# A steps with the scores first and the output projection's wait for y's low part moved to its second pass, in a hybrid attention layer on one core

## The chip, the cores and the metric

The kernel runs on one core of a Trainium2 chip. Times are microseconds (us) on the device, from the first to the last instruction of a launch with what lies around them. The profile is one execution; the median is that of three others.

## The reference

One layer with a sequence of 1024 tokens and a model width of 1024, all in float32. Cut to what is computed:

```
h  = rmsnorm(x, pre_g)
aq, ak, av, ag, bq, bk, bv, bg = split(h @ w_in)
# A: 8 heads of 64, keys shared by 4 heads, chunks of 64 tokens, each sees itself and the one before
s  = aq . ak * scale - slope * |i - j|        # masked before the start
ya = (softmax of [s, sink] without the sink's column) @ av * silu(ag)
# B: 4 heads with two softmax maps each, blocks of 128 queries, all keys up to their chunk
p  = softmax(bq . bk * scale - slope * |i - j|)
yb = rmsnorm((p[0] - lam * p[1]) @ bv, subln_g) * (1 - lambda_init) * silu(bg)
y  = concat(ya, yb) @ w_out
return x + rmsnorm(y, post_g)
```

## The kernel before

**Three passes.** Every projection in full precision is made of three products: high times high, low times high, high times low, where `x_hi` is x rounded to the TensorE's fp32r and `x_lo` the rest. ScalarE (ACT) makes the high parts by a copy, VectorE (DVE) or GpSimd (POOL) the low ones by a subtraction.

**Stages.** First x is normed, transposed and split into `hT_hi`, `hT_lo`, and the values of both groups are projected. Then comes the long middle: the 21 other column groups of `w_in` (the units: queries and keys of B, `qB` and `kB`, of A, `qA` and `kA`, and gates `gB`, `gA`) are projected in *pieces* of 4 matmuls of 512 columns, 6 pieces to a half unit of 512 tokens, and the attention is interleaved with these pieces. Last comes the output projection, tile by tile of 128 tokens, into 4 banks of PSUM, with norm, residual and store.

**One list orders all engines.** `make_schedule` writes one list of steps, `SCHEDULE`; each engine walks through that same list and issues its own instructions of each step, in that order, with waits on semaphores. So whatever step stands earlier in the list stands earlier in every engine's queue. The main loop goes over slots: 24 units of B, then the 8 units of A (slots 24 to 31), then the last 8 of B. In slot n stand the scores of unit n and the transposes and values of unit n - 1, "the pair one back". `take(k)` puts the next k pieces of projection into the list; `PIECES_BESIDE` says how many belong to a slot. When a piece ends a half unit, `store` is put there (ACT copies or activates the PSUM result), and the DVE's share (`store_low` for `qB` and `kB`, `gate` for the gates) waits in `later` until the next `vector_parts()`.

**A unit of A** is a pair of chunks, 2p and 2p + 1, called even and odd here:
- `a_scores`: PE makes 16 small matmuls (L1253); DVE adds the bias and takes the minimum, 8 operations (L1066) and one small one per chunk (L1073).
- `a_exp`: ACT, 4 exponentials of a chunk (L839) and one of the sink (L842).
- `a_weights`: DVE adds and inverts the sums (L1079, L1082), POOL multiplies the weights (L695).
- `a_transpose`: PE transposes a chunk's weights (L1261) into the half bank `turned`; ACT copies them out (L850). PE may only write the odd chunk's when ACT has copied the even one's (`turned_read`): there is one `turned`.
- `a_values`: PE (L1273), then DVE moves the result to `qT_A` (L1087).

**In a store** a half of `kB` costs ACT 4 copies (L781) and DVE 4 subtractions (L980), one of `qB` 2 and 2 (L773, L975), one of a gate one tanh (L794) and two products (L992, L999). The DVE's share waits for all ACT copies of that half. `split` is ACT's high part of the next unit's weights (L730).

**The end.** `y_split` makes y's high part on ACT (L860) and its low part on DVE (L1095). `out_project` (L1290) runs hi x hi, lo x hi, hi x lo.

Of the kernel before, what the change touches and what calls it, by code (L numbers as in the profile page):

```python
# [42 lines left out]
TILES = SEQ // P  # L43
# [29 lines left out]
PIECES = 6  # L73
# [5 lines left out]
Y_PARTS = 3  # L79
# [6 lines left out]

PIECES_BESIDE = ([9, 4, 3, 4, 4, 5, 3, 7] + [5, 5, 2, 3, 6, 5, 2, 8] + [5, 5, 3, 4, 3, 5, 3, 6]
                 + [6, 6, 6, 6, 6, 5, 5, 5]
                 + [4, 7, 7, 6, 3, 6, 5, 5] + [6, 1, 5])

SCORES_FIRST = {1, 2, 3, 10, 11, 17, 18, 37}
PIECE_BETWEEN = {16, 36, 37}
# [11 lines left out]
def make_schedule():  # L104

    steps, later, held = [], [], []
    pieces = [(n, half, p) for n in range(NU) for half in range(2) for p in range(PIECES)]
    at = 0

    def take(count):  # L110
        nonlocal at
        for n, half, p in pieces[at:at + count]:
            if half == 0 and p == 0 and n + 2 < NU:
                steps.append(("split", n + 2))
            steps.append(("project", n, half, p))
            if half == 0 and p < LOWS and n + 2 < NU:
                steps.append(("low", n + 2, p))
            if p < PIECES - 1:
                continue
            kind, head = UNITS[n]  # L120
            if kind == "kB" and head and ("b_scores", head * TILES - 1) not in steps:
                held.append((n, half))
            else:
                store(n, half)
        at = min(at + count, len(pieces))

    def store(n, half):


        steps.append(("store", n, half))  # L130
        if n not in PLAIN:
            later.append(("gate" if n in GATES else "store_low", n, half))

    def vector_parts():
        steps.extend(later)
        later.clear()

    order = [("b", u) for u in range(3 * TILES)] + [("a", p) for p in range(STEPS_A)]  # L140
    order += [("b", u) for u in range(3 * TILES, B_UNITS)]
    place = {unit: n for n, unit in enumerate(order)}
    turns = {}
    for unit, n in place.items():
        turns.setdefault(n + 1, []).insert(0, unit)

    steps += [("split", 0), ("split", 1)]
    take(FIRST_PIECES)
    vector_parts()
    for slot in range(len(order) + 3):  # L150
        kind, now = order[slot] if slot < len(order) else (None, None)
        count = PIECES_BESIDE[slot]
        last = order[slot - 1] if 0 < slot <= len(order) else (None, None)
        if last[0] == "b":
            steps.append(("b_mix", last[1]))
        before = order[slot - 2] if 2 <= slot < len(order) + 2 else (None, 0)
        finishing = before[0] == "b" and before[1] % 4 == 3
        if finishing:
            steps.append(("b_finish", before[1] // 4))
        if last[0] == "a":  # L160
            steps.append(("a_weights", 2 * last[1] + 1))
        turning = sorted(turns.get(slot, []))
        first = [("b_transpose", unit, 0) if which == "b" else ("a_transpose", 2 * unit)
                 for which, unit in turning[:1]]
        if kind == "b":
            assert {("kB", now // TILES), ("qB", now // TILES)} <= set(UNITS[:at // (2 * PIECES)])
            first.append(("b_scores", now))
        elif kind == "a":
            first.append(("a_scores", now))
        if slot in SCORES_FIRST:  # L170
            first.reverse()
        steps += first[:1]
        if slot in PIECE_BETWEEN and len(first) == 2:
            take(1)
            count -= 1
        steps += first[1:]
        vector_parts()
        for n, (which, unit) in enumerate(turning):
            if n:
                steps.append(("b_transpose", unit, 0))  # L180
            if which == "b" and unit % TILES >= 4:
                if n or kind is None:
                    take(1)
                    count -= 1
                steps.append(("b_transpose", unit, 1))
            if kind == "b" and n == len(turning) - 1:
                if now % TILES == TILES - 1:
                    for later_n, half in held:
                        store(later_n, half)
                    held.clear()  # L190
                steps.append(("b_exp", now))
            if which == "a":
                take(1)
                count -= 1
                if kind == "a":
                    steps.append(("a_exp", 2 * now))
                steps.append(("a_transpose", 2 * unit + 1))
            now_taken = 2 if which == "a" else 1 + finishing
            take(now_taken)
            count -= now_taken  # L200
            if kind == "a":
                if which == "b":
                    steps.append(("a_exp", 2 * now))
                steps += [("a_exp", 2 * now + 1), ("a_weights", 2 * now)]
            steps.append((f"{which}_values", unit))
            if which == "b" and unit % 4 == 3:
                steps.append(("b_square", unit // 4))
        if kind == "b" and not turning:
            steps.append(("b_exp", now))
        take(1)  # L210
        count -= 1
        vector_parts()
        if finishing:
            steps.append(("b_finish_transpose", before[1] // 4))
        take(max(0, count))
    last = (NU - 1) * 2 * PIECES
    outs = list(range(KT))
    while at < len(pieces):
        take(1)
        vector_parts()  # L220
        if outs and at % OUT_EVERY == 0:
            steps.append(("split_out", outs.pop(0)))
        if at == last + PIECES + 1:
            steps += [("y_split", 0), ("y_split", 1)]
    steps += [("split_out", k) for k in outs]
    for t in range(TILES):
        if t + 2 < TILES:
            steps.append(("y_split", t + 2))
        steps += [("out_project", t, 0), ("out_project", t, 1), ("post", t)]
    return steps  # L230
# [5 lines left out]
def hybrid_layer(nc, x, w_in, w_out, pre_norm_g, post_norm_g, sinks, lambda_q1, lambda_k1,  # L236
# [27 lines left out]
    a_weights = [place("a_weights0", 148.25, [P, 2, A_PAIRS, P]), place("a_weights1", 144.25, [P, 2, A_PAIRS, P])]  # L264
# [286 lines left out]
    with nc.Block() as block:  # L551
# [571 lines left out]
        def _(pe):  # L1123
# [51 lines left out]
            for step, *i in SCHEDULE:  # L1175
# [56 lines left out]
                elif step == "b_finish_transpose":  # L1232
                    f = i[0]
# [30 lines left out]
                elif step == "a_values":  # L1264
                    p = i[0]
                    pe.wait_ge(turned_read, turned_count("a_transpose", 2 * p + 1))
                    pe.wait_ge(mixed_read, mixed_before((step, *i)))
                    for e in range(2):
                        v = v_sb[:, p, B_WIDTH:V_WIDTH] if e else v_shift[:, p, :]
                        to = mixed[:, 256 * e:256 * e + 256]  # L1270
                        for h in range(2):
                            part = slice(HEAD_DIM * h, HEAD_DIM * (h + 1))
                            last = nc.tensor.matmul(to[part, :], v[:, part], a_weightsT[:, e, 2 * h:2 * h + 2, :],  # L1273
                                                    start=True, stop=True)
                    last.then_inc(a_valued, 1)
                elif step == "out_project":
                    t, half = i
                    tokens, cols = slice(P * t, P * t + P), slice(HALF * half, HALF * half + HALF)
                    pe.wait_ge(y_lo_ready, Y_PARTS * (t + 1))
                    if t >= 2:  # L1280
                        pe.wait_ge(y_weighted, 2 * (t - 2) + half + 1)
                    at = 1024 * (t % 2) + HALF * half
                    for p, (y, w) in enumerate(((hT_hi, wo_hi), (hT_lo, wo_hi), (hT_hi, wo_lo))):
                        for k in range(KT):
                            if t == 0 and half == 0 and p != 1:
                                if p:
                                    pe.wait_ge(wo_lo_ready[k % 2], k // 2 + 1)
                                else:
                                    pe.wait_ge(wo_hi_ready, k + 1)
                            last = nc.tensor.matmul(scores[:, at:at + HALF], y[:, k, tokens], w[:, k, cols],  # L1290
                                                    start=(p == 0 and k == 0), stop=(p == PASSES - 1 and k == KT - 1))
                    last.then_inc(out_projected, 1)
# [19 lines left out]
```

## Time and profile before

| | |
|---|---|
| median of 3 runs | 533.04 us (530.73 to 533.13) |
| profiled execution, its own time | 530.51 us |
| its span | 528.7 us |
| PE busy | 507.7 us, 96% |
| DVE busy | 263.5 us, 50% |
| ACT busy | 250.8 us, 47% |
| POOL busy | 115.6 us, 22% |
| TensorE's granted clock, mean | 0.995 |
| HBM read, written | 27.40 MB, 4.19 MB |

PE's busy time is close to the span, so the table says that work on PE, or a wait of PE, is what a change has to touch. It does not say where PE waits, nor what would be late next: for that the rows below are read, which show when each engine did what in a step of A and at the start of the output projection.

### The profile page before, as it was taken

To read this page: it belongs to the slowest core of one execution; us is meant where nothing else is said; L and a number is where in the kernel's file an instruction comes from. 1 tells how busy PE (TensorE), PEld (TensorE's weight loads), DVE (VectorE), ACT (ScalarE), POOL (GpSimd) and SP (SyncE) were. 2 spreads that over 40 slices of the span, in tenths; PEclk is the share of its full clock that TensorE was granted. 3 is DMA by queue.
4 is the path that set the end of the run, shared out by engine and by line. 5 is a ranking of instruction groups with operands and counts; after the bars stand their busy time and mean duration, and the time that the engine had idled before them with its cause. 6 is when DMAs were issued, how large, how long until landed. Compare 5 with 4: busy or idle time off the path is not lost.

```text
span 528.7 us, 7554 instructions
## 1 busy us (share of the span) xinstructions
PE 507.7 (96%) x2776; PEld 426.0 (81%) x2776; DVE 263.5 (50%) x642; ACT 250.8 (47%) x614; POOL 115.6 (22%) x154
## 2 busy tenths in 40 slices
PE   6999999999999999999999999989999999999995
PEld 5899997888878787888886767768788878888884
DVE  3656002465575556445547778445554475443332
ACT  5454213466476456556478666623645371221211
POOL 3410404040222120323043244222302260000000
PEclk9999999999999999999999999999999999999999
DMA  8730005120101110110101110111000653332222
GB/s 295 230 121 2 1 16 142 41 65 16 40 3 38 42 41 0 41 40 2 41 5 37 41 40 1 42 40 40 2 1 0 160 160 120 103 131 85 81 79 79
DMA packets 41300, 32.57 MB, mean 62 GB/s; under 512 B 18544, under 2 KB 35888, under 8 KB 41264
## 3 DMA queue, kind: packets, MB, share of 16 engines
q1 hardware_dynamic: 38960, 27.89, 18.9%
q10 hardware_dynamic: 2304, 4.20, 2.1%
q8 instruction: 22, 0.36, 0.3%
q14 instruction: 14, 0.11, 0.1%
HBM read 27.40 MB, written 4.19 MB: 60 GB/s over the span
## 4 chain that ended last, share of the span: by engine, by line
PE 80%; ACT 5%; DVE 4%; DMA 4%; issue 4%; POOL 2%; SPq 1%; DVEq 0%; POOLq 0%; ACTq 0%
PE proj L1188 35%; PE scores L1290 14%; PE proj L1158 10%; PE scores L1207 6%; PE banks L1228 5%; PE banks L1218 3%; DMA wo_early<-in_w_out 2%; PE banks L1273 2%; PE scores L1253 1%; PE banks L1261 1%; PE scores L1131 1%; DMA w_raw<-in_w_in 1%; DMA pre_g<-in_pre_norm_g 1%; ACT weights L801 1%; ACT k_stack L781 1%
## 5 line engine op out<-in xcount | busy, mean ns | idle before, releaser
L640 POOL TENSOR_TENSOR w_lo<-w_raw,w_hi 128x256 fp32r<-128x256 f32 x84 | 60.9, 754 | 184.8 <-ACT w_hi L730 184.8
L1188 PE MATMUL proj<-hT_hi,w_hi 128*128 128x512 f32 x336 | 89.9, 400 | 0.8 <-DVE k_stack L980 0.6
L1188 PE MATMUL proj<-hT_hi,w_lo 128*128 128x512 f32 x336 | 89.4, 400 | 0.0
L1188 PE MATMUL proj<-hT_lo,w_hi 128*128 128x512 f32 x336 | 88.5, 400 | 0.0
L1035 DVE CUSTOM_DVE_ANT_0 weights<-scores,dist_b 128x128 f32<-128x128 f32 (+7 forms) x64 | 45.9, 754 | 53.9 <-PE scores L1207 53.8
L1188 PEld LDWEIGHTS proj<-hT_hi,w_hi 128*128 128x128 f32 x336 | 60.5, 188 | 14.1 <-DVE k_stack L980 1.0
L1188 PEld LDWEIGHTS proj<-hT_hi,w_lo 128*128 128x128 f32 x336 | 60.6, 188 | 13.3 <-issue 1.9
L1188 PEld LDWEIGHTS proj<-hT_lo,w_hi 128*128 128x128 f32 x336 | 60.6, 188 | 11.8 <-issue 0.8
L801 ACT ACTIVATE weights<-weights,small 128x128 f32<-128x128 f32 (+7 forms) x64 | 49.0, 767 | 14.9 <-DVE small L1035 14.9
L811 ACT ACTIVATE weightsT<-banks 128x512 f32<-128x512 f32 (+3 forms) x48 | 23.6, 491 | 58.3 <-PE banks L1218 58.2
L1207 PE MATMUL scores<-k_stack,q_stack 128*128 128x512 f32 (+3 forms) x192 | 41.8, 353 | 0.0
L1228 PEld LDWEIGHTS banks<-v_sb,weightsT 128*128 128x128 f32 x288 | 36.2, 191 | 4.5 <-ACT weightsT L811 1.9
L1228 PE MATMUL banks<-v_sb,weightsT 128*128 128x128 f32 x288 | 37.8, 276 | 0.1
L644 POOL TENSOR_TENSOR small<-small 128x1 f32<-128x1 f32 (+1 forms) x24 | 17.2, 717 | 87.1 <-DVE small L1108 85.7
L1207 PEld LDWEIGHTS scores<-k_stack,q_stack 128*128 128x128 f32 x192 | 31.9, 189 | 4.8 <-DVE k_stack L980 0.4
L870 ACT ACTIVATE banks<-scores 128x512 f32<-128x512 f32 x16 | 9.3, 582 | 54.7 <-PE scores L1290 54.7
L1290 PE MATMUL scores<-wo_hi,hT_hi 128*128 128x512 f32 x128 | 31.7, 390 | 1.3 <-DVE hT_lo L1095 1.3
L1019 DVE SCALAR_TENSOR_TENSOR weights<-weights,small,weights 128x512 f32<-128x512 f32 (+3 forms) x48 | 31.1, 676 | 1.1
L1290 PE MATMUL scores<-wo_lo,hT_hi 128*128 128x512 f32 x128 | 31.6, 389 | 0.0
L1290 PE MATMUL scores<-wo_hi,hT_lo 128*128 128x512 f32 x128 | 31.6, 389 | 0.0
L1066 DVE CUSTOM_DVE_ANT_0 a_weights<-scores,dist_a,small 128x128 f32<-128x128 f32 x64 | 22.5, 406 | 17.9 <-PE scores L1253 17.9
L1290 PEld LDWEIGHTS scores<-wo_hi,hT_hi 128*128 128x128 f32 x128 | 23.9, 188 | 6.6 <-DVE hT_lo L1095 1.7
(106 smaller groups left out, 721.8 us busy)
## 6 DMA issues: line engine op xcount, KB each, us to landing
w_raw<-in_w_in SPq DMA_DIRECT2D x13, 512.0 KB, 3.9
x_in<-in_x SPq DMA_DIRECT2D x8, 512.0 KB, 5.9
w_raw<-in_w_in SPq DMA_DIRECT2D x16, 256.0 KB, 3.5
x_res<-in_x SPq DMA_DIRECT2D x8, 512.0 KB, 4.4
out<-y_out ACTq DMA_DIRECT2D x16, 256.0 KB, 2.3
wv_raw<-in_w_in SPq DMA_DIRECT2D x2, 640.0 KB, 7.4
wo_early<-in_w_out SPq DMA_DIRECT2D x4, 256.0 KB, 4.9
w_raw<-in_w_out SPq DMA_DIRECT2D x4, 256.0 KB, 6.2
```

Source lines behind the costliest of these rows:

```text
L640: nc.gpsimd.tensor_tensor(w_lo[:, n % SPLIT, k], w_raw[:, n % RAW, k], w_hi[:, n % SPLIT, k].bitcast(F32), ALU.subtract).then_inc(w_lo_rea ...
L644: nc.gpsimd.tensor_tensor(out_, in_, neg_half[:, 0:width], ALU.pow).then_inc(done, 1)
L801: nc.scalar.activation(w, w, ACT.Exp, scale=-1.0, bias=min_b[:, 2 * u + m:2 * u + m + 1], accum_out=sum_b[:, 2 * u + m:2 * u + m + 1]).the ...
L811: nc.scalar.activation(weightsT[:, 4 * r:4 * r + blocks, :], turned[:, 0:P * blocks].rearrange("p (b q) -> p b q", q=P), ACT.Copy).then_in ...
L1019: nc.vector.scalar_tensor_tensor(w0, w1, mix_b[:, u:u + 1], w0, ALU.mult, ALU.add).then_inc(b_mixed, 1)
L1035: nc.vector.tensor_tensor_reduce(out=weights_1[:, 0:keys] if m else weights_0[:, u % 2, 0:keys], in0=scores[:, 1024 * m:1024 * m + keys], ...
L1066: nc.vector.tensor_tensor_reduce(out=a_weights_of(c)[:, j, :], in0=scores[:, a_scores_at(c, j):a_scores_at(c, j) + P], in1=dist_a[:, min(c ...
L1158: last = nc.tensor.matmul(proj[:, n % 2, 0:VG], h[:, k, tokens], w[:, k, cols], start=(p == 0 and k == 0), stop=(p == PASSES - 1 and k == ...
L1188: last = nc.tensor.matmul(to, w[:, slot, k, :], h[:, k, HALF * half:HALF * half + HALF], start=(p == 0 and k == first), stop=(p == PIECES ...
L1207: last = nc.tensor.matmul(scores[:, 1024 * m + first:1024 * m + first + width], q_stack[head][m][:, P * block_:P * block_ + P], k[:, m, fi ...
L1228: last = nc.tensor.matmul(mixed[:, P * (u % 4):P * (u % 4) + P], weightsT[:, b, :], v_sb[:, b, P * head:P * head + P], start=(b == 0), sto ...
L1290: last = nc.tensor.matmul(scores[:, at:at + HALF], y[:, k, tokens], w[:, k, cols], start=(p == 0 and k == 0), stop=(p == PASSES - 1 and k ...
```

## The change

In slots whose transposes are those of an A unit (25 to 32), the list is written in another order. Before: transposes of the even chunk, scores of the new unit, the vector parts, a piece, exp of the new even chunk, transposes of the odd chunk, two pieces, exp of the new odd chunk, values, a piece, vector parts, other pieces. Now: scores, vector parts, two pieces, exp of the new even chunk, transposes of the even chunk, a piece, transposes of the odd chunk, exp of the new odd chunk, a piece, values, a piece, vector parts, other pieces. The count of pieces of a slot stays, but for one that moves from slot 33 to slot 32. In the output projection the wait for `y_lo_ready` stands at the second pass; the first waits for `y_hi_ready`.

```diff
-                 + [4, 7, 7, 6, 3, 6, 5, 5] + [6, 1, 5])
+                 + [5, 6, 7, 6, 3, 6, 5, 5] + [6, 1, 5])
...
+        if turning and turning[0][0] == "a":
+            done = turning[0][1]
+            steps.append((f"{kind}_scores", now))
+            vector_parts()
+            take(2)
+            steps += [("a_exp", 2 * now) if kind == "a" else ("b_exp", now), ("a_transpose", 2 * done)]
             take(1)
-            count -= 1
...
+            steps.append(("a_transpose", 2 * done + 1))
+            if kind == "a":
+                steps += [("a_exp", 2 * now + 1), ("a_weights", 2 * now)]
+            take(1)
+            steps.append(("a_values", done))
+            count -= 4
+        else:
...
-            if which == "a":
...
-                if kind == "a":
-                    steps.append(("a_exp", 2 * now))
-                steps.append(("a_transpose", 2 * unit + 1))
-            now_taken = 2 if which == "a" else 1 + finishing
...
                 elif step == "out_project":
...
-                    pe.wait_ge(y_lo_ready, Y_PARTS * (t + 1))
+                    pe.wait_ge(y_hi_ready, Y_PARTS * (t + 1))
...
                     for p, (y, w) in enumerate(((hT_hi, wo_hi), (hT_lo, wo_hi), (hT_hi, wo_lo))):
+                        if p == 1:
+                            pe.wait_ge(y_lo_ready, Y_PARTS * (t + 1))
```

The new code's line numbers are 4 higher on all engines in the middle stage (L980 is L984, L1066 is L1070), and 6 higher in the output projection.

The first place is the DVE's queue around the first half of unit 12, the keys of B's last head. Before, in slots 27 and 28 (from the end of the scores of unit 3 to the start of those of unit 4):

```order
L1073 TENSOR_TENSOR small<-small 128x4
L980 TENSOR_TENSOR k_stack<-proj,k_stack 64x512 x4
L1079 TENSOR_TENSOR small<-small 128x4
L1082 RECIPROCAL small<-small 128x4
L1087 TENSOR_SCALAR qT_A<-banks 128x2x256
L1079 TENSOR_TENSOR small<-small 128x4
L1082 RECIPROCAL small<-small 128x4
L1066 ISA a_weights_61,small<-scores,dist_a,small 128x128
```

The same operations of this half unit now, from the end of the scores of unit 2 to the start of those of unit 3:

```order
L1077 TENSOR_TENSOR small<-small 128x4
L1083 TENSOR_TENSOR small<-small 128x4
L1086 RECIPROCAL small<-small 128x4
L1091 TENSOR_SCALAR qT_A<-banks 128x2x256
L984 TENSOR_TENSOR k_stack<-proj,k_stack 64x512 x4
L1083 TENSOR_TENSOR small<-small 128x4
L1086 RECIPROCAL small<-small 128x4
L1070 ISA a_weights_62,small<-scores,dist_a,small 128x128
```

The four subtractions stood behind a slot's score operations (before) and stand now, a whole slot's score operations earlier, ahead of the odd chunk's inversion and of the scores of unit 3 (its weights lie in `a_weights_62`).

The second place is ACT's queue in the same slots, 27 and the start of 28. Before:

```order
L781 ACTIVATE k_stack<-proj 64x512 x4
L850 ACTIVATE a_weightsT<-banks 128x512
L839 ACTIVATE a_weights_62,small<-a_weights_62,small 128x128 x4
L842 ACTIVATE small<-small 128x4
L850 ACTIVATE a_weightsT<-banks 128x512
L839 ACTIVATE a_weights_62,small<-a_weights_62,small 128x128 x4
```

And now:

```order
L785 ACTIVATE k_stack<-proj 64x512 x4
L843 ACTIVATE a_weights_62,small<-a_weights_62,small 128x128 x4
L846 ACTIVATE small<-small 128x4
L854 ACTIVATE a_weightsT<-banks 128x512 x2
L843 ACTIVATE a_weights_62,small<-a_weights_62,small 128x128 x4
L846 ACTIVATE small<-small 128x4
```

Both copies of the transposed weights now stand behind the new unit's even exponentials; before, the even one stood ahead of them.

The third place is PE's queue in that slot, its projection pieces of 4 matmuls with it. Before:

```order
L1261 MATMUL banks<-ident,a_weights_61 128x128 x4
L1253 MATMUL scores<-kT_A,qT_A 128x128 x8
L1188 MATMUL proj<-hT_hi,w_hi 128x512 x4
L1261 MATMUL banks<-ident,a_weights_61 128x128 x4
L1188 MATMUL proj<-hT_lo,w_hi 128x512 x8
L1273 MATMUL banks<-a_weightsT,v_shift 64x256 x2
```

And now:

```order
L1257 MATMUL scores<-kT_A,qT_A 128x128 x8
L1192 MATMUL proj<-hT_hi,w_hi 128x512 x4
L1192 MATMUL proj<-hT_lo,w_hi 128x512 x4
L1265 MATMUL banks<-ident,a_weights_61 128x128 x4
L1192 MATMUL proj<-hT_lo,w_hi 128x512 x4
L1265 MATMUL banks<-ident,a_weights_61 128x128 x4
L1192 MATMUL proj<-hT_hi,w_lo 128x512 x4
L1277 MATMUL banks<-a_weightsT,v_shift 64x256 x2
```

The scores no longer stand between the two sets of transposes, and the distance from the odd chunk's transposes to the values is one piece instead of two.

## Rows read from the trace of the kernel before

**Rows 1.** The page's engine line of PE: busy us, share of the span, instructions.

```profile
PE 507.7 (96%) x2776; PEld 426.0 (81%) x2776; DVE 263.5 (50%) x642; ACT 250.8 (47%) x614; POOL 115.6 (22%) x154
```

**Rows 2.** Who PE waited for, 262 to 350 us: total, times, longest.

```profile
PE banks L1218 <- DVE weights L1019: 2.1, 1, 2.1
PE banks L1261 <- POOL a_weights L695: 1.9, 3, 1.2
PE banks L1273 <- ACT a_weightsT L850: 0.5, 1, 0.5
```

**Rows 3.** Timeline of PE, slots 27 and 32: start, us, what.

```profile
293.03 1.08 PE L1188 MATMUL proj<-hT_hi,w_hi 128*128 128x512 f32 x4
293.95 0.60 PE L1261 MATMUL banks<-ident,a_weights 128*128 128x128 f32 x4
294.48 1.26 PE L1253 MATMUL scores<-kT_A,qT_A 64*128 64x128 f32 x16
...
296.70 0.60 PE L1261 MATMUL banks<-ident,a_weights 128*128 128x128 f32 x4
297.05 2.09 PE L1188 MATMUL proj<-hT_lo,w_hi 128*128 128x512 f32 x8
299.07 0.65 PE L1273 MATMUL banks<-a_weightsT,v_shift 128*64 128x256 f32 x4
...
338.88 0.60 PE L1261 MATMUL banks<-ident,a_weights 128*128 128x128 f32 x4
339.24 0.64 PE L1207 MATMUL scores<-k_stack,q_stack 128*128 128x128 f32 x4
```

**Rows 4.** Timeline of DVE, slot 27, and the gate in slot 29.

```profile
295.89 0.41 DVE L1066 CUSTOM_DVE_ANT_0 a_weights<-scores,dist_a,small 128x128 f32<-128x128 f32 x1 [2.91 <-PE scores L1253]
...
298.95 2.84 DVE L980 TENSOR_TENSOR k_stack<-proj,k_stack 64x512 fp32r<-64x512 f32 x4
301.82 0.16 DVE L1079 TENSOR_TENSOR small<-small 128x4 f32<-128x4 f32 x1
...
302.23 0.69 DVE L1087 TENSOR_SCALAR qT_A<-banks 128x512 f32<-128x512 f32 x1
...
319.09 0.68 DVE L992 SCALAR_TENSOR_TENSOR gate<-gate,proj 128x512 f32<-128x512 f32 x1
...
320.42 0.15 DVE L1079 TENSOR_TENSOR small<-small 128x4 f32<-128x4 f32 x1
```

**Rows 5.** Timeline of ACT, slots 27, 29 and 32.

```profile
293.23 2.44 ACT L781 ACTIVATE k_stack<-proj 64x512 fp32r<-64x512 f32 x4 [2.61 <-PE proj L1188]
...
296.34 0.40 ACT L839 ACTIVATE a_weights<-a_weights,small 128x128 f32<-128x128 f32 x1
...
298.00 0.57 ACT L850 ACTIVATE a_weightsT<-banks 128x512 f32<-128x512 f32 x1
...
313.13 0.60 ACT L794 ACTIVATE gate<-proj 128x512 f32<-128x512 f32 x1 [2.63 <-PE proj L1188]
...
339.58 0.60 ACT L850 ACTIVATE a_weightsT<-banks 128x512 f32<-128x512 f32 x1 [2.09 <-PE banks L1261]
...
342.76 1.05 ACT L730 ACTIVATE w_hi<-w_raw 128x1024 fp32r<-128x1024 f32 x1
```

**Rows 6.** Timeline of POOL, slot 27.

```profile
302.27 1.04 POOL L695 TENSOR_TENSOR a_weights<-a_weights,small 128x512 f32<-128x512 f32 x1 [8.18 <-DVE small L1082]
```

**Rows 7.** Timeline of all engines where the output projection starts.

```profile
432.51 1.98 PE L1188 MATMUL proj<-hT_hi,w_lo 128*128 128x512 f32 x8
...
434.59 1.04 ACT L763 ACTIVATE wo_hi<-w_raw 128x1024 fp32r<-128x1024 f32 x1
435.02 0.68 DVE L1095 TENSOR_TENSOR hT_lo<-out_B,hT_hi 128x512 fp32r<-128x512 f32 x1
...
435.76 2.11 PE L1290 MATMUL scores<-wo_hi,hT_hi 128*128 128x512 f32 x8 [1.27 <-DVE hT_lo L1095]
...
436.90 1.21 DVE L1003 TENSOR_TENSOR wo_lo<-w_raw,wo_hi 128x1024 fp32r<-128x1024 f32 x1
```

More of the change, by code:

```diff
@@ L162, in make_schedule @@
         turning = sorted(turns.get(slot, []))
[L163 to L172, printed above, removed]
@@ L173, in make_schedule @@
-        if slot in PIECE_BETWEEN and len(first) == 2:
-            take(1)
-            count -= 1
[L176 to L191, printed above, removed]
-            if which == "a":
+        if turning and turning[0][0] == "a":
[4 more added lines that the diff above has]
+            steps += [("a_exp", 2 * now) if kind == "a" else ("b_exp", now), ("a_transpose", 2 * done)]
+            take(1)
+            steps.append(("a_transpose", 2 * done + 1))
[5 more added lines that the diff above has]
+        else:
+            first = [("b_transpose", unit, 0) for which, unit in turning[:1]]
+            if kind == "b":
+                assert {("kB", now // TILES), ("qB", now // TILES)} <= set(UNITS[:at // (2 * PIECES)])
+                first.append(("b_scores", now))
+            elif kind == "a":
+                first.append(("a_scores", now))
+            if slot in SCORES_FIRST:
+                first.reverse()
+            steps += first[:1]
+            if slot in PIECE_BETWEEN and len(first) == 2:
@@ L193, in make_schedule @@
                 take(1)
                 count -= 1
-                if kind == "a":
-                    steps.append(("a_exp", 2 * now))
-                steps.append(("a_transpose", 2 * unit + 1))
-            now_taken = 2 if which == "a" else 1 + finishing
-            take(now_taken)
-            count -= now_taken
-            if kind == "a":
-                if which == "b":
-                    steps.append(("a_exp", 2 * now))
-                steps += [("a_exp", 2 * now + 1), ("a_weights", 2 * now)]
@@ L205, in make_schedule @@
-            steps.append((f"{which}_values", unit))
-            if which == "b" and unit % 4 == 3:
-                steps.append(("b_square", unit // 4))
+            steps += first[1:]
+            vector_parts()
+            for n, (which, unit) in enumerate(turning):
+                if n:
+                    steps.append(("b_transpose", unit, 0))
+                if which == "b" and unit % TILES >= 4:
+                    if n or kind is None:
+                        take(1)
+                        count -= 1
+                    steps.append(("b_transpose", unit, 1))
+                if kind == "b" and n == len(turning) - 1:
+                    if now % TILES == TILES - 1:
+                        for later_n, half in held:
+                            store(later_n, half)
+                        held.clear()
+                    steps.append(("b_exp", now))
+                take(1 + finishing)
+                count -= 1 + finishing
+                if kind == "a":
+                    steps += [("a_exp", 2 * now), ("a_exp", 2 * now + 1), ("a_weights", 2 * now)]
+                steps.append((f"{which}_values", unit))
+                if which == "b" and unit % 4 == 3:
+                    steps.append(("b_square", unit // 4))
```

## The prediction

> **What bounds the kernel now.** I read the page first: PE is busy for 507.7 of 528.7 us [rows 1], so only a change of PE's work or of its waits moves the end. The other engines matter as what PE waits for. Then I asked the view of waits who PE waits for in the stretch of the A steps, 262 to 350 us [rows 2]: three waits for POOL's multiplied weights (1.9 us), one for ACT's copy of the transposed weights (0.5), one for the DVE's mixed weights of unit 24 (2.1). At the start of the output projection PE sits idle for 1.27 us until `hT_lo` is there [rows 7]. So 1.9 + 0.5 + 1.3 = 3.7 us is the most that the change can take away, unless it shortens PE's work, which it does not: the matmuls are the same. The 2.1 us before the transposes of unit 24 stay, because between the values of unit 7 and those transposes the list has one piece before and after, and the DVE's queue there is the same.
>
> **PE's clock through one new A slot.** I lay out a slot with 0 at the start of its scores, from the timelines. Before, scores and the piece behind them took 296.70 - 294.48 = 2.22 us, a plain piece 293.95 - 293.03 = 0.92, transposes 297.05 - 296.70 = 0.35, and a piece between two switches (299.07 - 297.05) / 2 = 1.01 [rows 3]. In the new order the even chunk's transposes start at 2.22 + 0.92 = 3.14, the odd chunk's at 3.14 + 0.35 + 1.01 = 4.50, the values at 4.50 + 0.35 + 1.01 = 5.86. Before, the odd chunk's transposes came at 2.22 and the values at 4.59.
>
> **The chain that must keep up.** The DVE starts the bias operations 295.89 - 294.48 = 1.41 after the scores start, if it is free [rows 3, 4]. ACT's first exponential starts 0.45 behind (296.34), and the chunk's five take 298.00 - 296.34 = 1.66 [rows 4, 5]. In the new list ACT has both copies of the transposed weights behind those exponentials; a copy takes 0.57 to 0.60, and starts 339.58 - 338.88 = 0.70 after its transposes [rows 3, 5]. PE may start the odd transposes only when the even copy is done. With a free DVE: exponentials done at 1.41 + 0.45 + 1.66 = 3.52, copy 3.84 to 4.44, odd transposes on time at 4.50. So the order just closes. Its slack is small: the odd transposes are late once the bias starts later than 4.50 - 0.05 (semaphore, chosen) - 0.57 - 1.66 - 0.45 = 1.77, or once anything else holds ACT past 3.9. From there every us of lateness is a us of PE idle, since nothing can pass in PE's queue.
>
> **What is late: the halves of kB.** Call E the issue of the group behind the last piece of a half unit. ACT begins the store at E + 0.20 (293.03, 293.23) and takes 2.44 for `kB` [rows 3, 5], so to E + 2.64. The DVE's four subtractions take 301.82 - 298.95 = 2.87 and the inversion 302.23 - 301.82 = 0.41 [rows 4]. In the new queue both stand ahead of the next scores: bias at E + 2.67 + 2.87 + 0.41 = E + 5.95. The next scores start one piece behind E, about E + 0.95, so the bias starts at 5.00 instead of 1.41, the exponentials end at 7.11, the copy at 7.68, and the odd transposes start at 7.73 instead of 4.50: **3.2 us** of idle PE. POOL's multiplication of the odd chunk (1.04 us, [rows 6]) ends about 6.1, inside that. Unit 12 is `kB`, with two halves stored in this stretch, in slots 26 and 27: 6.4 us in slots 27 and 28. Before, these subtractions stood behind the bias operations, where they delayed only the inversion of chunks that PE wanted later; what that cost is in [rows 2].
>
> **The other slots.** A gate's half takes ACT 0.60 and the DVE 320.42 - 319.09 = 1.33 [rows 4, 5]. With a piece between store and scores (slot 29) the bias starts at E + 0.83 + 1.33 + 0.41 = E + 2.57, or 1.62: inside the slack. In slot 30 no piece lies between, so the bias is at 2.57; ACT's exponentials start at 3.02 (the tanh, 0.60, and `w_hi`, 1.05, [rows 5], are over by 1.9), end at 4.68, and the odd transposes start at 5.30: 0.8 lost. In slot 31 a store lies between scores and exponentials; the tanh starts at 2.2 + 0.2 and pushes the exponentials' end to about 4.6 and the odd transposes to 5.2: 0.7. In slot 32 the same happens with scores of B, which are shorter (339.24, 0.64 of matmul time, [rows 3]), and `split` 17 stands between the two copies: 0.9. The `qB` half before slot 26 has half the operations of a `kB` half: bias near 1.9, 0.1 lost. Slots 24 and 25: nothing. Sum of new waits in A: 6.4 + 0.8 + 0.7 + 0.9 + 0.1 = 8.9.
>
> **What it removes.** The waits of [rows 2] for POOL and ACT, 2.4: multiplication and copy have a longer lead now.
>
> **Switching costs on PE.** Transposes directly before scores took 294.48 - 293.95 = 0.53, before a piece 0.35 [rows 3]: a switch from 128-row to 64-row operands costs about 0.18. The new order has that switch too, from a piece to the scores, and one more neighbourhood of a piece and transposes (1.01 against 0.92, 0.09). A piece ahead of scores does not occur in this trace. From below it costs no more than today's switch, 0; from above I take the 0.35 that the transposes themselves last, once per slot. I choose 0.5 us for the eight slots in all; ends 0 and 2.8. The Trainium skill, page "TensorEngine Tiling (Array Packing)", section "Key Properties", says that changing the tiling mode drains the TensorE. It gives no figure; the trace agrees that such a switch costs something (those 0.18 us), and behind the longer matmuls of a piece a drain would cost more than behind transposes, which is the upper end.
>
> **The output projection.** PE's last group before it starts at 432.51, and its eight matmuls issue in two plain pieces of 0.92, so PE is free at 432.51 + 1.84 = 434.35 [rows 3, 7]. The first pass needs y's high part, which must be over when its low part is being made, and `wo_hi`'s eight chunks; the last is ready at 434.59 + 1.04 = 435.63, and PE gets to it at 434.35 + 7 x 0.23 = 435.96. The second pass starts at 434.35 + 1.84 = 436.19; y's low part is ready at 435.02 + 0.68 = 435.70. `wo_lo`'s last chunk, 436.90 + 1.21 = 438.1, is wanted at 434.35 + 2 x 1.84 + 1.61 = 439.6 [rows 7]. All three covers hold, the first by 0.3 us only. Gain: 435.76 - 434.35 = **1.4**; ends 0.9 (chunk 7 late) and 1.4. Behind this PE runs to the end without a wait, so the gain stays.
>
> **Sum.** 8.9 + 0.5 - 2.4 - 1.4 = +5.6 us. Against the profiled execution's own 530.5 that is 536.1; the median of the runs shown is 2.5 higher, at 533.04, so I forecast 538.6 for the median. The stage behind A moves as a whole: its loads and stores wait on PE's own progress.
>
> **The rivals.**
> - *Faster.* The transposes' lead over their scores grows by a third, all waits of A go, and nothing takes their place: +0.5 - 2.4 - 1.4 = -3.3, 529.7. For it: the plain chain closes at 4.44 against 4.50. Against it: it needs the bias to start by 1.77 in every slot, and the DVE's queue puts the `kB` subtractions ahead. It would decide if those were done by E + 2.3, where even ACT's copies end at E + 2.64. Chance 0.09.
> - *Within 0.5%.* 0.5% is about what a measurement of this kernel can tell from no change, 2.7 us. The two `kB` waits come out at half and the small ones not at all: 3.2 + 0.5 - 2.4 - 1.4 = 0, 533; up to +2.6. For it: the small terms rest on a few tenths each. Against it: the `kB` chain is made of durations that hardly vary in the trace. Chance 0.13.
> - *The drain.* As forecast, but each scores block behind a piece costs the upper end: +2.3 more, 540.9. Chance 0.10.
> - *The output projection gains nothing*, because y's high part or chunk 7 comes as late as the low part did: +1.4, 540.0. The rows speak against it; chance 0.06.
> - The forecast, +3 to +7.5: chance 0.62.
>
> **How the numbers follow.** Faster 0.09, within 0.5% 0.13, slower 0.78 (0.62 + 0.10 + 0.06). The range: from a case with `kB` waits at half and one or two small ones (533.5, which takes in half of the middle case) to the forecast with the switching end (542). Left out: the faster case, the lower part of the middle one, and a little above.
>
> **What would show it.** In the new profile: the DVE's L984 x4 ahead of L1070 in slots 27 and 28 and its scores operations some 5 us behind PE's scores; PE idle about 3 us before L1265 twice, released by ACT's copy L854; under 1 us before L1265 three times; no wait for POOL; the stretch from the first A scores to the transposes of unit 24 longer by about 7 us; L1296 with no idle before it, and 1.4 us less between the last projection and the end. Wrong would be: no idle at L1265 (then the DVE's order does not reach PE), or idle before the scores L1257 themselves.

## The result and the profile after

| | before | changed |
|---|---|---|
| median of 6 runs each, same chip | 533.09 us | 539.84 us |
| lowest to highest | 530.73 to 533.23 | 537.86 to 540.85 |
| profiled execution, own time | 530.51 us | 537.86 us |
| its span | 528.7 us | 536.1 us |

The ratio is 1.0134, with a 95% interval of 1.0106 to 1.0162. It compares the means of the runs, which lie 7.1 us apart; the medians lie 6.75 apart and the two profiled executions 7.4. The forecast was 5.6 slower, a median of 538.6, with a range of 533.5 to 542.0.

The page's engine line of the changed kernel, beside [rows 1]:

```profile
PE 510.8 (95%) x2776; PEld 427.1 (80%) x2776; DVE 260.2 (49%) x642; ACT 250.5 (47%) x614; POOL 115.1 (21%) x154
```

The number of instructions is the same, but PE's busy time grew by 3.1 us. So not all of the loss is waiting; some matmuls took longer. Who PE waited for, in the whole run (total, times, longest), beside [rows 2], which cover the A stretch alone; of the second line here only the longest wait, 1.7, lies in that stretch:

```profile
PE banks L1265 <- ACT a_weightsT L854: 8.3, 5, 3.2
PE banks L1222 <- DVE weights L1023: 3.0, 4, 1.7
```

The row of POOL's multiplied weights is gone, and in its place stands ACT's copy of the transposed weights, five times. The timeline of PE in slots 26 and 27, beside [rows 3]:

```profile
289.04 0.63 PE L1265 MATMUL banks<-ident,a_weights 128*128 128x128 f32 x4
289.43 1.17 PE L1192 MATMUL proj<-hT_hi,w_lo 128*128 128x512 f32 x4
290.53 0.65 PE L1277 MATMUL banks<-a_weightsT,v_shift 128*64 128x256 f32 x4
...
292.58 1.07 PE L1192 MATMUL proj<-hT_hi,w_hi 128*128 128x512 f32 x4
293.58 1.26 PE L1257 MATMUL scores<-kT_A,qT_A 64*128 64x128 f32 x16
...
297.08 1.18 PE L1192 MATMUL proj<-hT_lo,w_hi 128*128 128x512 f32 x4
301.50 1.09 PE L1265 MATMUL banks<-ident,a_weights 128*128 128x128 f32 x4 [3.24 <-ACT a_weightsT L854]
302.24 2.06 PE L1192 MATMUL proj<-hT_hi,w_lo 128*128 128x512 f32 x4
304.22 0.93 PE L1277 MATMUL banks<-a_weightsT,v_shift 128*64 128x256 f32 x4
...
307.55 1.26 PE L1257 MATMUL scores<-kT_A,qT_A 64*128 64x128 f32 x16
```

Two things are to be seen. The odd transposes wait 3.24 us, released by ACT's copy. And behind the wait the same four matmuls take 2.06 us instead of 1.17: from the odd transposes to the next scores it is 307.55 - 301.50 = 6.05 us in slot 27 and 293.58 - 289.04 = 4.54 in slot 26, 1.51 more. The stretches' view says why; its columns are PE's busy time with its matmuls, then the weight loads, DVE, ACT, POOL, then the granted clock:

```profile
293.58:307.55 13.97, 10.73 (x57) 7.61 (x56) 7.11 (x27) 6.93 (x25) 2.08 (x2) 0.88 0.01 2
307.55:321.39 13.84, 10.61 (x57) 7.55 (x56) 7.47 (x28) 7.69 (x25) 4.87 (x6) 0.88 0.18 38
...
301.50:304.50 3.00, 3.00 (x10) 2.16 (x12) 0.41 (x3) 1.82 (x8) 1.04 (x1) 0.50 0.02 5
```

In slots 27 and 28 the granted clock is 0.88 on average, and 0.50, that is 1.2 GHz, right behind the wait. PE had been idle since 298.3; the clock was still 1.00 from 300 to 301, 0.91 from 301.0 to 301.5, and back at 1.00 from 305.0. The DVE and ACT in slot 27, beside [rows 4, 5], show where the wait comes from:

```profile
295.25 2.85 DVE L984 TENSOR_TENSOR k_stack<-proj,k_stack 64x512 fp32r<-64x512 f32 x4 [2.90 <-ACT k_stack L785]
298.13 0.16 DVE L1083 TENSOR_TENSOR small<-small 128x4 f32<-128x4 f32 x1
...
298.53 0.41 DVE L1070 CUSTOM_DVE_ANT_0 a_weights<-scores,dist_a,small 128x128 f32<-128x128 f32 x1
```

```profile
292.77 2.44 ACT L785 ACTIVATE k_stack<-proj 64x512 fp32r<-64x512 f32 x4 [0.78 <-PE proj L1192]
298.99 0.40 ACT L843 ACTIVATE a_weights<-a_weights,small 128x128 f32<-128x128 f32 x1 [3.77 <-DVE small L1070]
...
300.76 0.60 ACT L854 ACTIVATE a_weightsT<-banks 128x512 f32<-128x512 f32 x1
302.68 0.60 ACT L854 ACTIVATE a_weightsT<-banks 128x512 f32<-128x512 f32 x1 [1.33 <-PE banks L1265]
```

The scores start at 293.58 and their bias at 298.53, 4.95 later (forecast 5.00). ACT sits idle for 3.77 us in front of exponentials that stand ahead of a copy whose transposes have long been done. Where the output projection starts, beside [rows 7]:

```profile
440.41 0.69 DVE L1003 TENSOR_TENSOR out_B<-gate,out_B 128x512 f32<-128x512 f32 x1
440.51 2.85 POOL L683 TENSOR_TENSOR wo_lo<-w_raw,wo_hi 128x1024 fp32r<-128x1024 f32 x1 [1.82 <-ACT wo_hi L767]
...
441.40 1.98 PE L1192 MATMUL proj<-hT_hi,w_lo 128*128 128x512 f32 x8
441.64 2.33 DVE L1099 TENSOR_TENSOR hT_lo<-qT_A,hT_hi 128x256 fp32r<-128x256 f32 x2 [0.55 <-ACT hT_hi L864]
...
443.21 1.98 PE L1296 MATMUL scores<-wo_hi,hT_hi 128*128 128x512 f32 x8
```

Its first matmul follows 1.81 behind the start of the last group, against 435.76 - 432.51 = 3.25 before: 1.44 gained.

### The profile page after: what moved, and what is told of

It reads as the page before. It is cut to its first block, busy times and chain, and to the rows that moved or that the text cites. A ratio compares the mean times of both kernels' runs of the same rounds, so it can differ in the third digit from the quotient of the medians.

```text
span 536.1 us, 7554 instructions
## 1 busy us (share of the span) xinstructions
PE 510.8 (95%) x2776; PEld 427.1 (80%) x2776; DVE 260.2 (49%) x642; ACT 250.5 (47%) x614; POOL 115.1 (21%) x154
## 4 chain that ended last, share of the span: by engine, by line
PE 82%; ACT 6%; DVE 5%; issue 4%; DMA 2%; POOL 1%; SPq 0%; DVEq 0%; POOLq 0%; ACTq 0%
PE proj L1192 37%; PE scores L1296 14%; PE proj L1162 10%; PE scores L1211 6%; PE banks L1232 5%; PE banks L1222 3%; PE banks L1277 2%; DVE k_stack L984 2%; PE banks L1265 1%; ACT k_stack L785 1%; PE scores L1135 1%; PE scores L1257 1%; ACT a_weights L843 1%; DMA pre_g<-in_pre_norm_g 1%; DMA w_raw<-in_w_in 1%
## 5 line engine op out<-in xcount | busy, mean ns | idle before, releaser
L1192 PE MATMUL proj<-hT_hi,w_lo 128*128 128x512 f32 x336 | 92.1, 407 | 0.0
L1192 PE MATMUL proj<-hT_lo,w_hi 128*128 128x512 f32 x336 | 89.7, 400 | 0.0
L984 DVE TENSOR_TENSOR k_stack<-proj,k_stack 64x512 fp32r<-64x512 f32 x32 | 22.0, 688 | 18.2 <-ACT k_stack L785 17.5
L843 ACT ACTIVATE a_weights<-a_weights,small 128x128 f32<-128x128 f32 x64 | 24.8, 390 | 12.1 <-DVE small L1070 12.1
```

What stands on the lines that cost most here:

```text
L843: nc.scalar.activation(w, w, ACT.Exp, scale=-1.0, bias=min_a[:, s + j:s + j + 1], accum_out=sum_a[:, s + j:s + j + 1]).then_inc(a_exped, 1)
L984: nc.vector.tensor_tensor(k_lo[part, m, tokens], source[own, :], k_hi[own, m, tokens].bitcast(F32), ALU.subtract).then_inc(stack_lo, 1)
L1192: last = nc.tensor.matmul(to, w[:, slot, k, :], h[:, k, HALF * half:HALF * half + HALF], start=(p == 0 and k == first), stop=(p == PIECES ...
```

## The experiments

The ratios compare means with runs of the kernel before that were made beside the experiment's: 23 for experiments 1 to 4 (median 532.31 us), 17 for experiments 5 to 7 (532.32). The numbers of this section are the order in which the experiments are told.

**1. The DVE's share of a store behind the next scores again.**

```diff
         take(1)
         count -= 1
-        vector_parts()
+        if not (turning and turning[0][0] == "a"):
+            vector_parts()
```

> The changed kernel, but in slots that turn an A unit the DVE's share of a store is held back until behind the next scores, as it stood before the change. My theory (the DVE's queue order makes the two long waits, and the clock falls behind them): the two 3.2 us waits before the odd transposes go, and with them the stretches at a lower granted clock that follow them, about 1.5 us each; slot 30's 0.5 us goes too, slots 31 and 32 keep 0.6 each because there the store stands between scores and exponentials. Some 0.5 us may come in slot 28, where ACT has four k_stack copies and w_hi ahead of the exponentials. Together 9.4 to 9.9 us less than the changed kernel, so 530.0 to 530.5, ratio to before 0.994 to 0.996. Rival (scores first is itself dear, by the switch from a piece to 64-row scores and the short way from odd transposes to values): the waits shrink by less than half, ratio above 1.003.

Measured: 528.74 us (median of 6, 526.66 to 529.0), ratio to before 0.9925 (0.9901 to 0.9949). The profile's span is 524.9 us, 11.2 below the changed kernel. Its granted clock is 1.00 through the A stretch. Who PE waited for:

```profile
PE banks L1223 <- DVE weights L1024: 1.6, 4, 0.7
PE banks L1266 <- ACT a_weightsT L855: 1.6, 3, 0.7
```

One move of the DVE's instructions turns the change from slower than before to faster. Both long waits are gone; 0.30, 0.60 and 0.65 us are left before the odd transposes of slots 28, 31 and 32, as the theory had it. In the profiles it gained 11.2 us, where 9.4 to 9.9 were expected. Some 1.3 us of that were not in the theory: the wait before the transposes of unit 24 fell from 1.74 us to 0.42, because a gate's two products, 0.68 and 0.69 us on the DVE, no longer stand ahead of that unit's mix. The rival, scores first as such, is out.

**2. Both copies of the transposed weights ahead of the even exponentials.** The DVE's order stays as in the change.

```diff
-            steps += [("a_exp", 2 * now) if kind == "a" else ("b_exp", now), ("a_transpose", 2 * done)]
+            steps.append(("a_transpose", 2 * done))
             take(1)
             steps.append(("a_transpose", 2 * done + 1))
+            steps.append(("a_exp", 2 * now) if kind == "a" else ("b_exp", now))
```

> The changed kernel, but the even exponentials of the new unit stand behind both transposes of the old one in the list, so ACT copies the transposed weights first. The DVE's order stays as changed. My theory: the lateness reaches PE through two links, ACT's exponentials ahead of the copy (odd transposes possible at 7.7 us into the slot) and POOL's multiplication of the odd chunk (ends about 6.1 us into the slot). With the first link cut the second is left: 1.2 us of idle before the odd transposes in slots 27 and 28 each, released by POOL and not by ACT, and the small waits of slots 30 to 32 gone. If a wait of 1.2 us leaves the granted clock alone, 4.1 + 1.8 + 2.9 = 8.8 us less than the changed kernel: 531.0, ratio to before 0.996; if the clock still falls, 533.9, ratio 1.001. Rival (the DVE's lateness reaches PE by POOL alone, ACT's order does not matter): same as the changed kernel, ratio 1.013.

Measured: 533.13 us (median of 10), ratio 1.0025 (1.0009 to 1.0042), 5.8 us below the changed kernel's 1.0134. PE's waits in the two slots, from its timeline:

```profile
300.16 0.66 PE L1266 MATMUL banks<-ident,a_weights 128*128 128x128 f32 x4 [2.16 <-POOL a_weights L700]
...
312.40 0.66 PE L1266 MATMUL banks<-ident,a_weights 128*128 128x128 f32 x4 [1.41 <-POOL a_weights L700]
```

The theory's sign and place hold: ACT's link is cut, POOL's is left, and the small waits of slots 30 to 32 are gone. The rival that POOL alone carries the lateness is out. The size was missed: 2.16 and 1.41 us instead of 1.2 twice. Part of it is that ACT now does the exponentials later, which pushed the `kB` copies to 293.27, and the DVE's subtractions with them to 295.73, 2.41 us after the scores' start (1.67 in the changed kernel). The granted clock was 0.59 behind the longer wait and 1.00 behind the shorter one:

```profile
300.00:304.00 4.00, 3.84 (x16) 2.21 (x16) 2.43 (x16) 2.80 (x13) 0.20 (x2) 0.59 0.03 6
312.00:316.00 4.00, 3.60 (x21) 2.45 (x22) 3.07 (x19) 2.84 (x14) 2.55 (x5) 1.00 0.05 11
```

**3. The output projection's wait alone**, on the kernel before: only the last hunk of the change.

```diff
-                    pe.wait_ge(y_lo_ready, Y_PARTS * (t + 1))
+                    pe.wait_ge(y_hi_ready, Y_PARTS * (t + 1))
...
+                        if p == 1:
+                            pe.wait_ge(y_lo_ready, Y_PARTS * (t + 1))
```

> The kernel before with only the output projection's wait moved to its second pass. My theory: PE has no idle before the first matmul of the output projection, and 1.4 us less: 531.7, ratio 0.9973 (0.9968 to 0.998). Rival (something behind it gives it back, the y_weighted wait or the last norm): ratio 1.000.

Measured: 531.12 us (median of 12), ratio 0.9977 (0.9961 to 0.9993). A gain, but the profiled execution does not show it: its span is 528.8 us against 528.7 of the kernel before. It has waits that the theory did not have:

```profile
430.90 2.42 POOL L679 TENSOR_TENSOR wo_lo<-w_raw,wo_hi 128x1024 fp32r<-128x1024 f32 x1 [0.92 <-ACT wo_hi L763]
430.99 0.67 DVE L992 SCALAR_TENSOR_TENSOR gate<-gate,proj 128x512 f32<-128x512 f32 x1
431.70 2.18 DVE L999 TENSOR_TENSOR out_B<-gate,out_B 128x512 f32<-128x512 f32 x1
433.97 0.73 ACT L860 ACTIVATE hT_hi<-qT_A 128x256 fp32r<-128x256 f32 x2 [3.14 <-DVE out_B L999]
...
435.27 1.89 PE L1292 MATMUL scores<-wo_hi,hT_hi 128*128 128x512 f32 x7 [0.59 <-ACT hT_hi L860]
437.35 0.50 PE L1292 MATMUL scores<-wo_hi,hT_hi 128*128 128x512 f32 x1 [0.20 <-ACT wo_hi L763]
```

The DVE's product `out_B<-gate,out_B` takes 0.69 us in the changed kernel's profile and 2.18 here, where POOL's subtraction had begun 0.8 us ahead of it; it ends 0.56 us after POOL's does. In the changed kernel it began 0.10 us ahead of POOL's, and it was the DVE's next operations that took long (2.33 us for two, against 0.76 where POOL is quiet). So the high part of y comes early or late by which of the two engines is first. In the profiles of the kernel before, the changed kernel and experiment 1, the product began 0.06 to 0.14 us ahead of POOL; in those of experiments 2, 3, 4 and 5 POOL began 0.12 to 0.80 us ahead, and the product took 2.18 to 2.82 us. In experiment 3's profile the second pass starts 437.69 - 432.70 = 4.99 us behind the start of the last group, against 437.70 - 432.51 = 5.19 before, so only 0.2 us were gained there, and the first A scores had come 0.2 us later.

**4. The idle time filled**, to price the clock. The changed kernel computes what it did; 13 matmuls are added whose results nobody reads.

```diff
+                    if c in (5, 7):
+                        p = c // 2
+                        pe.wait_ge(a_biased, 2 * A_PAIRS * (p + 1))
+                        for f in range(FILL):          # FILL = 13
+                            nc.tensor.matmul(scores[:, 1024 * (p % 2):1024 * (p % 2) + HALF], hT_hi[:, f % KT, 0:P],
+                                             hT_hi[:, f % KT, 0:HALF], start=True, stop=True)
                     pe.wait_ge(a_weighted, c + 1)
```

> The changed kernel with 13 matmuls of 512 columns that nobody reads put on PE before the odd transposes in slots 27 and 28, where PE sits idle for 3.2 us; they write a bank of scores that is free then. The reads and waits of all else stay. My theory: the two waits cost more than their idle time, because the granted clock is lower behind them (0.88 over each slot); 13 matmuls take about 2.95 us and keep PE busy, so the granted clock stays at 1.00, the idle that is left is 0.3 us, and each slot is about 1.4 us shorter: 2.9 us less than the changed kernel, 537.0, ratio to before 1.007 to 1.008. Rival (the slow matmuls behind a wait have another reason, such as a pipeline that fills again, or the clock falls with them too): no gain, ratio 1.013 or more.

Measured: 537.0 us (median of 4), ratio 1.0091 (1.0059 to 1.0122), where the changed kernel has 1.0134. The two slots, and then a stretch 36 us further on:

```profile
293.78:306.24 12.46, 12.18 (x71) 9.06 (x70) 7.11 (x27) 6.94 (x25) 2.08 (x2) 1.00 0.01 2
306.24:318.70 12.46, 12.18 (x71) 9.05 (x70) 7.47 (x28) 7.70 (x25) 4.89 (x6) 1.00 0.19 42
354.40:358.40 4.00, 3.92 (x14) 3.44 (x15) 1.72 (x8) 1.37 (x5) 0.00 (x0) 0.57 0.51 112
```

The wait ends when it did, and yet the slots take 12.46 us each instead of 13.97 and 13.84: 1.51 and 1.38 less, 2.9 together, with the clock at 1.00. More work on PE made the slots shorter, and the added matmuls, with their wait, are the only difference between the two kernels. The Trainium skill, page "TensorE: Matmul & The Clock Gate", section "Part 1: The HAM clock gate", names two levels of the clock, 1.2 GHz when idle and 2.4 GHz when busy. The rows agree on the levels, 0.50 behind the idle stretch and 1.00 where it is filled; they also show that the lower level came at the end of the idle stretch and lay mostly over the busy work behind it. By the profile alone this kernel is not faster than the changed one (spans 537.0 and 536.1), because in that execution the clock fell behind the 1.74 us wait before unit 24 (from there to the last projection group 85.84 us against 84.23), and the high part of y came late as in the third experiment (3.22 us from the last group to the output projection against 1.81, and 0.6 more behind it); the ratio of the timed runs is what the gain is taken from: 2.3 us, by the two intervals uncertain by about 2 either way. The price of the clock rests on the slots' rows.

**5. The first two edits together.**

> The changed kernel with the edits of the first two experiments together: the DVE's share of a store stands behind the next scores, and ACT copies both sets of transposed weights ahead of the even exponentials. My theory: with the DVE on time again, the waits left in the A stretch are those where a store or w_hi on ACT stands ahead of the exponentials (0.3, 0.6 and 0.65 us before the odd transposes in the version with the first edit alone); with the copies ahead of the exponentials they go, so 1.5 us less than that version's 528.7: 527.2, ratio to before 0.9895 to 0.990. Rival: ACT now begins the exponentials near the end of the slot and falls behind (in the version with the second edit alone, its k_stack copies began 0.5 us later): new waits for POOL's multiplied weights take their place, ratio 0.992 or more.

Measured: 528.83 us (median of 6), ratio 0.993 (0.9905 to 0.9955). The theory's gain over experiment 1 did not come. PE's waits:

```profile
PE scores L1298 <- ACT hT_hi L866: 1.3, 1, 1.3
...
PE banks L1267 <- ACT a_weightsT L856: 0.8, 1, 0.8
PE banks L1267 <- POOL a_weights L701: 0.6, 1, 0.6
```

Three small waits (1.55 us) have become two (1.4): in slot 28 the odd transposes wait for POOL (0.62), as the rival had it. From the first A scores to the transposes of unit 24 it is 80.49 us here and 80.32 in experiment 1, so with the DVE on time ACT's order shows no gain.

**6. POOL's subtraction held back**, on experiment 3.

```diff
                     pool.wait_ge(wo_hi_ready, k + 1)
+                    if k == 6:
+                        pool.wait_ge(gated, 2 * len(GATES) - 1)
```

> The kernel before with the output projection's wait moved, as in the third experiment, and POOL's last subtraction for wo_lo held back until the DVE has done the gate product of the last unit's first half. My theory: in the third experiment that product took 2.18 us and not 0.69, because POOL's subtraction (2.42 us) had begun just before it, and the high part of y came 1.4 us late for it; which of the two starts first differs from execution to execution. With POOL held back the product takes 0.69 us every time, PE has no idle before the first matmul of the output projection, and the gain is the whole 1.4 us: ratio to before 0.996 to 0.997, and the profile shows the product at 0.69 us with L1095 at above 1 us behind it. Rival (the long product has another cause, or POOL's later subtraction makes the third pass late): as in the third experiment, 0.9977, or slower.

Measured: 530.25 us (median of 12), ratio 0.9962 (0.9944 to 0.998). The rows on which the reading rests:

```profile
433.17 0.69 DVE L1001 TENSOR_TENSOR out_B<-gate,out_B 128x512 f32<-128x512 f32 x1
434.41 2.62 DVE L1097 TENSOR_TENSOR hT_lo<-qT_A,hT_hi 128x256 fp32r<-128x256 f32 x2 [0.55 <-ACT hT_hi L862]
```

```profile
434.17 1.98 PE L1190 MATMUL proj<-hT_hi,w_lo 128*128 128x512 f32 x8
435.98 1.98 PE L1294 MATMUL scores<-wo_hi,hT_hi 128*128 128x512 f32 x8
```

As expected, the product is short, the low parts are long, and PE goes on without a gap, 1.81 us from group to group. The Trainium skill, page "SBUF — State Buffer", section "SBUF: two separate sides", calls the port pair that VectorE and GpSimd share an exclusive lock, held for the whole instruction by whichever starts first, where the VectorE's has two SBUF inputs and the GpSimd's reads SBUF. The rows of experiments 3 and 6 agree: 2.18 against 0.69 us for one product, while the operation `gate<-gate,proj`, with one of its inputs in PSUM, took 0.67 us beside POOL's in experiment 3. Against experiment 3 the intervals overlap (0.9961 to 0.9993 and 0.9944 to 0.998), so the size rests on the profiles and on the next run. The profile's span, 528.8 us, is again no shorter than before: the 1.4 us gained at the output projection were lost behind the wait before unit 24, where the clock fell in this execution (86.54 us from there to the last projection group, against 85.14 before).

**7. All of it**: experiments 5 and 6 on the changed kernel. The expectation counts in another order: its "fourth" is experiment 5 here.

> The fourth and sixth edits on the changed kernel together. My theory: the gains add up, because they lie 90 us apart and nothing between has slack to swallow them: 0.5 us below the fourth, or as fast where its executions happened to be in the good order; 526.8, ratio to before 0.989. Its executions should also lie closer together than the 2.3 us of the first experiment, if the order of the DVE's and POOL's operations there is what splits them. Rival: no difference to the fourth experiment and the same spread.

Measured: 527.03 us (median of 6), ratio 0.9901 (0.9879 to 0.9923). Its six executions lie between 526.84 and 527.22, 0.38 us apart; those of experiment 1 lie 2.3 us apart and those of experiment 5 2.5. The only difference to experiment 5 is POOL's wait, and it is worth 1.8 us at the median, more than the 0.5 expected. The one profile of experiment 5 is in the order with POOL first; that most of its other executions were too would explain the size, but they have no profile. This version has the lowest median, 1% below the kernel before, though its interval overlaps that of experiment 1, whose two fastest executions (526.66 and 526.68) are a little shorter. Part of the output projection's gain is not there: its eighth matmul waits for the last chunk of `wo_hi`,

```profile
433.94 0.50 PE L1300 MATMUL scores<-wo_hi,hT_hi 128*128 128x512 f32 x1 [0.20 <-ACT wo_hi L771]
```

and the first pass takes 434.29 - 431.91 = 2.38 us, against 445.04 - 443.21 = 1.83 in the changed kernel.

## Why the prediction was right, and where it was off

**The chain** was right in its mechanism, and the two waits of 3.2 us came as 3.24 and 3.23, released by ACT's copy, with the bias at 4.95 instead of 5.00. That the waits agree to some hundredths is partly luck: the odd transposes came 7.92 after the scores' start and not 7.73, and on time (slots 25 and 29) they come at 4.59 and not 4.50, and these two errors nearly cancel. Experiment 1 takes away what was said to be late, and both go; experiment 2 cuts ACT's link and leaves POOL's, so there are two by which the lateness reaches PE. POOL's was sized too early: it let PE go 300.16 - 293.32 = 6.84 into the slot, where the prediction had its end at about 6.1.

**The other slots** were sized a little too high: 0.53, 0.60 and 0.65 us in slots 30 to 32 where 0.8, 0.7 and 0.9 stood, and nothing in slot 26 where 0.1 stood. Sum of new waits 8.25 (forecast 8.9).

**What it removes** was right: no wait for POOL and none before the values.

**The switching costs** (0.5, ends 0 and 2.8) were close to the lower end. A piece ahead of the scores takes 293.58 - 292.58 = 1.00 against 0.92 plain, 0.08 more. The rival of the drain is out.

**The 2.1 us that were to stay** became 1.74: the gate's product ahead of unit 24's mix took the DVE 0.69 us and not 1.02, so the queue there was the same but not its durations.

**What was missing is the clock.** The prediction said that from the point of lateness "every us of lateness is a us of PE idle", and priced nothing behind it. Each 3.2 us wait was followed by some 3 us at a granted clock of 0.50, which cost 1.5 and 1.4 us: 2.9 in all, measured by rows of the changed kernel and again by experiment 4. The step that failed is that sentence: the price of a wait is its length plus what the clock costs behind it. In the profiled executions the A stretch then adds up as 8.25 - 2.4 - 0.3 + 2.9 = 8.4 of the 8.7 us that it grew, measured from the first A scores to unit 24's transposes and less one moved piece of 0.92; the 0.3 left are small switches. The sum of the prediction for that stretch was 7.0. The missing 2.9 were partly offset by new waits, switches and the wait before unit 24 that were each sized a little too high; the rest fell into the upper part of the range, which had been left there for switching costs and not for the clock.

**The output projection** gave 1.44 in that profile, as forecast. That this holds in each execution was wrong: the cover "y's high part must be over when its low part is being made" has a case where POOL stands in its way, and the gain is then less. The third experiment's profile shows 0.59 + 0.20 us of idle in its place. The lower end of 0.9, for chunk 7 of `wo_hi` being late, is what experiment 7's profile shows: PE starts on time, 1.44 less, but the first pass is 0.55 longer.

## What to carry to other kernels

When steps are reordered in a list that all engines share, follow each engine's queue on its own: here PE's order got better, and what cost the time was four DVE subtractions that came to stand ahead of the DVE's operations on fresh scores. Price a new wait on TensorE with what follows it: look at the granted clock behind the waits in several traces, since here waits of one length were followed by either level. Where a kernel's executions fall into two groups, look for two engines' operations that begin within some tenths of a us of each other and last longer when the other is first. Here a wait that fixes their order was worth 1.8 us at the median, and the executions lay 0.38 us apart instead of 2.5.

## What was not expected of the hardware

The granted clock fell behind some short waits and not behind others of the same length. The wait of 2.07 us before unit 24's transposes left it at 1.00 in the kernel before and in experiment 3, and in experiment 6, with the same 2.07 us, it was 0.57 over 4 us:

```profile
347.63 0.48 PE L1220 MATMUL banks<-ident,weights 128*128 128x128 f32 x1 [2.07 <-DVE weights L1021]
347.76 1.20 PE L1209 MATMUL scores<-k_stack,q_stack 128*128 128x256 f32 x4
348.76 1.91 PE L1190 MATMUL proj<-hT_lo,w_hi 128*128 128x512 f32 x4
```

```profile
347.00:351.00 4.00, 3.37 (x12) 2.99 (x13) 1.95 (x9) 1.37 (x5) 0.39 (x1) 0.57 0.60 131
```

The same happened with 1.74 us: 1.00 in the changed kernel, 0.57 in experiment 4. A fall behind such a wait cost 86.54 - 85.14 = 1.4 us in experiment 6 and 85.84 - 84.23 = 1.6 in experiment 4. What decides whether the clock falls is left open; no run here was made for it. Behind the waits of 3.24 and 3.23 us the clock fell both times, behind one of 1.41 us it did not. This, and the two orders of POOL and DVE, are what the runs show that could spread the times of one kernel: the kernel before, with such a wait and the order left free, spreads over 3.8 and 4.7 us in its two sets of runs, experiment 1 with only the free order over 2.3, experiment 6 with only the wait of 2.07 us over 3.0, and experiment 7 with neither over 0.4. A smaller part lies ahead of the A steps: in the nine profiles the granted clock from 10 to 20 us was 0.66 to 1.00, and the first A scores started between 265.41 and 266.15. That these are the whole of the spread is argued, not shown.
